# A decoder layer on one core: 15 instead of 11 units of seven block products in the down projection, their row sums formed earlier, residual rows parked in DRAM

## The reference

```
h = h + rmsnorm(merged @ w_out, post_mix_g)          # residual rows, 256 x 2048
u = rmsnorm(h, pre_ffn_g)
ff = (silu(u @ w_gate) * (u @ w_up)) @ w_down        # 2048 -> 5632 -> 2048
h = h + rmsnorm(ff, post_ffn_g)
return h[:, N_META:]                                 # 256 x 2048
```

## Time and profile before

| | |
|---|---|
| median of 3 runs | 1106.71 us (1106.59 to 1107.04) |
| the profiled execution | 1106.06 us |
| its span, first to last instruction | 1104.1 us |
| PE busy | 1090.2 us, 99% |
| DVE busy | 764.0 us, 69% |
| ACT busy | 546.8 us, 50% |
| DMA | 203.52 MB, mean 184 GB/s |
| feed-forward stage, from the first block to the down stage | 368 to 861 us |
| down stage, half 0 | 861 to 978 us |
| down stage, half 1, with the tail | 978 to 1104 us |

### The profile page before, as it was taken

One profiled execution on the slowest core, in us unless ns is written; L12 is line 12 of the kernel. 1 busy time (PEld: TensorE's weight loads), 2 busy tenths in 40 slices (PEclk: granted clock), 3 DMA queues, 4 the chain that ended last, 5 costly groups with the idle time before them and its releaser, 6 DMA issues.

```text
span 1104.1 us, 17760 instructions
## 1 busy us (share of the span) xinstructions
PE 1090.2 (99%) x6479; PEld 968.0 (88%) x6479; DVE 764.0 (69%) x939; ACT 546.8 (50%) x677; POOL 27.3 (2%) x46
## 2 busy tenths in 40 slices
PE   9999999999999999999999999999999999999996
PEld 8999999999888888888888888888888888888885
DVE  6699896546747866666666656666666788787676
ACT  6544544746544754444444444444444455555452
POOL 4001001001000000000000000000000000000000
PEclk9999999999999999999999999999999999999999
DMA  8655445534486376566656666666666656656662
GB/s 279 204 180 162 148 136 152 154 96 153 148 310 191 116 248 190 173 203 190 191 173 198 188 190 184 188 192 190 189 178 197 194 186 205 220 170 215 198 202 95
DMA packets 154847, 203.52 MB, mean 184 GB/s; under 512 B 6305, under 2 KB 133729, under 8 KB 154033
## 3 DMA queue, kind: packets, MB, share of 16 engines
q1 hardware_dynamic: 153616, 197.29, 57.8%
q10 hardware_dynamic: 608, 4.20, 0.9%
q0 software_dynamic: 576, 1.40, 0.4%
HBM read 200.77 MB, written 2.10 MB: 184 GB/s over the span
## 4 chain that ended last, share of the span: by engine, by line
PE 95%; DVE 3%; ACT 1%; issue 0%; DVEq 0%; POOL 0%; ACTq 0%; POOLq 0%
PE ps L1304 29%; PE ps L1306 15%; PE ps L1289 6%; PE ps L1291 5%; PE ps L1292 5%; PE ps L1675 5%; PE ps L1676 5%; PE ps L1677 5%; PE ps L1585 3%; PE ps L1587 3%; PE ps L1586 3%; PE ps L1700 2%; PE ps L1701 2%; PE ps L1702 2%; DVE w_lo L849 1%; PE ps L1443 1%
## 5 line engine op out<-in xcount | busy, mean ns | idle before, releaser
L849 DVE TENSOR_TENSOR w_lo<-raw,w_hi 128x1024 fp32r<-128x1024 f32 x357 | 434.7, 1229 | 252.9 <-ACT w_hi L494 252.2
L494 ACT ACTIVATE w_hi<-raw 128x1024 fp32r<-128x1024 f32 x357 | 375.4, 1059 | 398.0 <-PE ps L1306 253.9
L1304 PE MATMUL ps<-u,w_hi 128*128 128x512 f32 x1408 | 491.1, 392 | 0.8 <-DVE u L957 0.8
L1306 PE MATMUL ps<-u,w_lo 128*128 128x256 f32 x1408 | 395.0, 281 | 0.0
L1304 PEld LDWEIGHTS ps<-u,w_hi 128*128 128x128 f32 x1408 | 264.0, 188 | 60.3 <-issue 1.1
L1306 PEld LDWEIGHTS ps<-u,w_lo 128*128 128x128 f32 x1408 | 265.3, 188 | 0.0
L1289 PE MATMUL ps<-u,w_hi 128*128 128x272 f32 (+1 forms) x544 | 158.8, 292 | 0.0
L1291 PE MATMUL ps<-u,w_hi 128*128 128x272 f32 (+1 forms) x544 | 155.9, 287 | 0.0
L1292 PE MATMUL ps<-u,w_lo 128*128 128x272 f32 (+1 forms) x544 | 155.7, 286 | 0.0
L1675 PE MATMUL ps<-w_hi,ffn 128*128 128x512 f32 x264 | 102.8, 389 | 1.5 <-DVE w_lo L849 1.5
L1289 PEld LDWEIGHTS ps<-u,w_hi 128*128 128x128 f32 x544 | 102.4, 188 | 0.4
(11 more groups left out here) (236 smaller groups left out, 919.3 us busy)
## 6 DMA issues: line engine op xcount, KB each, us to landing
raw<-in_w_gate SPq DMA_DIRECT2D x88, 512.0 KB, 4.6
raw<-in_w_up SPq DMA_DIRECT2D x88, 512.0 KB, 4.5
raw<-in_w_down SPq DMA_DIRECT2D x88, 512.0 KB, 4.7
raw<-in_w_in SPq DMA_DIRECT2D x72, 512.0 KB, 3.6
raw<-in_w_out SPq DMA_DIRECT2D x32, 512.0 KB, 4.5
arena<-in_x SPq DMA_DIRECT2D x2, 1024.0 KB, 6.1
arena<-in_x ACTq DMA_DIRECT2D x2, 1024.0 KB, 8.3
out<-f_acc SPq DMA_DIRECT2D x3, 512.0 KB, 2.7
```

The costliest lines, as they stand in the source:

```text
L494: act.activation(w_hi[:, slot, :], raw[:, slot, :], ACT.Copy).then_inc(hi_done, 1)
L849: dve.tensor_tensor(w_lo[:, slot, :], raw[:, slot, :], hi_view(w_hi[:, slot, :]), ALU.subtract).then_inc(lo_done, 1)
L1304: pe.matmul(ps[:, bank + m, :].rearrange("p (a t) -> p a t", a=2), w_hi[:, slot, at], u[:, kt, :, 0:SEQ], start=first and k == 0, stop=Fal ...
L1306: mm = pe.matmul(ps[:, bank + m, 0:SEQ], w_lo[:, slot, at], u[:, kt, 0, 0:SEQ], start=False, stop=last and k == len(kts) - 1, skip_group_c ...
```

## The change

It has four parts.

1. Which units are seven units, and in what order the units of a half are worked. A string for each half (ROUND, P plain, Z seven) now gives the order, and the list TURNS the unit at each place. Half 0 has seven seven units (before: 5), half 1 has eight (before: 6). Before, they stood at every third place. Now they stand at places 2, 5, 8, 11, 14, 17, 19 of half 0 and 3, 5, 7, 9, 11, 13, 16, 18 of half 1 (places from 0; a place is two chunks). Between most there are two plain units; between 17 and 19 of half 0, and in half 1 between 3, 5, 7, 9, 11, 13 and between 16, 18, there is one.
2. The row sums of units 8 to 12 are made inside feed-forward blocks 8 to 12, from the float32 product tile, in a new tile sums_y. Three sums (units 13, 14, 15) are left in the down stage, before six.
3. sums_y lies over h2rows. The residual rows are therefore written to the output tensor in DRAM (2 MB, two DMAs on ACT's queue) before feed-forward block 1, and read back (two DMAs of 1 MB on SP's queue) when the last seven unit has ended. The load of gbc moves from the beginning of the feed-forward stage to its end.
4. fold_sums stands at place FOLD[n] + 4: 43 in half 0 and 41 in half 1, before 42 in both. SP's loads of w_down are written out, not in a loop.

The core of the diff:

```
-    SEVEN_D = (3, 6, 9, 12, 15, 18)
-    SEVEN_0 = (6, 9, 12, 15, 18)
-    SUM_AT = {4: 6, 9: 9, 15: 12, 21: 15, 27: 18, 33: 3}
+    Y0, Y1 = 8, 13
+    SEVEN_Y, SEVEN_U = tuple(range(Y0, Y1)), (13, 14, 15)
+    SUM_AT = {13: 13, 19: 14, 25: 15}
     SUM_NO = {d: i for i, d in enumerate(SUM_AT.values())}
-    SEVENS = [(n, d) for n in range(DW) for d in (SEVEN_D if n else SEVEN_0)]
+    ROUND = ("PPZPPZPPZPPZPPZPPZPZPP", "PPPZPZPZPZPZPZPPZPZPPP")
+    def in_turn(n):
+        sevens = list(SEVEN_Y + SEVEN_U)[:ROUND[n].count("Z")]
+        plain = [d for d in range(FT // 2) if d not in sevens]
+        return [(sevens if c == "Z" else plain).pop(0) for c in ROUND[n]]
+    TURNS = [in_turn(n) for n in range(DW)]
+    SEVENS = [(n, d) for n in range(DW) for d, c in zip(TURNS[n], ROUND[n]) if c == "Z"]
     SEVEN_NO = {nd: z for z, nd in enumerate(SEVENS)}
     SEVENS_TO = [sum(1 for k, _ in SEVENS if k <= n) for n in range(DW)]
+    SEVEN_END = [ROUND[n].rindex("Z") for n in range(DW)]
     QUARTERS = [(0, 0), (0, 1), (1, 0), (1, 1)]
-    FOLD = 2 * max(SEVEN_D) + 2
-    assert FOLD <= DCH - LAST and 0 not in SEVEN_D and DW == 2
+    FOLD = [2 * SEVEN_END[n] + 1 for n in range(DW)]
...
-        sums = sb_at("sums", [P, len(SEVEN_D), 3, 2, P], F32R, a_sums)
-        assert 4 * NQ * WIDE <= 24 * P * len(SEVEN_D) <= a_in + 8 * KT * TOK - a_sums
+        sums = sb_at("sums", [P, len(SEVEN_U), 3, 2, P], F32R, a_sums)
...
+        y_f = sb_at("y_f", [P, 1, 4, P], F32, a_xt)
...
+        sums_y = sb_at("sums_y", [P, Y1 - Y0, 3, 2, P], F32R, a_y)
...
-            with sp_eng.Fori(0, DW) as i:
-                for kt in range(DCH):
-                    load(wd_v, kt, i * WIDE, i * DCH + (Q_DOWN + kt), kt % WSLOTS, kts=1, cols=WIDE)
+            for n in range(DW):
+                for e in range(DCH):
+                    q = Q_DOWN + n * DCH + e
+                    load(wd_v, 2 * TURNS[n][e // 2] + e % 2, n * WIDE, q, q % WSLOTS, kts=1, cols=WIDE)
+            sp_eng.wait_ge(h2_kept, 16 * NQ)
+            sp_eng.wait_ge(t_used, len(SEVENS))
+            for m in range(NQ):
+                sp_eng.dma_start(h2rows[:, m, :], out_v[:, m, :]).then_inc(h2_back[m], 16)
...
-            act.wait_ge(y_sq, NQ * DN)
-            act.wait_ge(yg_done, NQ * DN)
-            act.dma_start(gbc[:, :], post_ffn_g.to_broadcast([P, D])).then_inc(gbc_landed, 16)
...
+            act.wait_ge(rows_done, NQ * DN)
+            for m in range(NQ):
+                act.dma_start(out_v[:, m, :], h2rows[:, m, :]).then_inc(h2_kept, 16)
...
+            with act.Fori(1, Y0) as i:
+                gate_part(i)
+                up_part(i, range(CK, 2 * CK))
+            act.wait_ge(h2_kept, 16 * NQ)
+            with act.Fori(0, Y1 - Y0) as j:
+                gate_part(j + Y0)
+                up_part(j + Y0, range(CK, CK + 2))
+                act.wait_ge(y_step, j * 4 + 4)
+                act.copy(sums_y[:, bass.ds(j, 1), :, 0, :], y_f[:, :, 0:3, :]).then_inc(y_hi, 1)
+                act.copy(ffn[:, bass.ds(j * 2 + 2 * Y0, 1), 0, P:SEQ], y_f[:, 0, 3:4, :]).then_inc(y_hi, 1)
+                up_part(j + Y0, range(CK + 2, 2 * CK))
+            with act.Fori(Y1, NFB - 1) as i:
+                gate_part(i)
+                up_part(i, range(CK, 2 * CK))
+            act.wait_ge(y_lo, 2 * (Y1 - Y0))
+            act.dma_start(gbc[:, :], post_ffn_g.to_broadcast([P, D])).then_inc(gbc_landed, 16)
...
+            def product_sums(j):
+                a11, a12, a21, a22 = (tmp_ffn[:, 3, k * SEQ + m * P:k * SEQ + (m + 1) * P] for m in range(2) for k in range(2))
+                dve.tensor_tensor(y_f[:, 0, 0, :], a21, a22, ALU.add).then_inc(y_step, 1)
+                dve.tensor_tensor(y_f[:, 0, 3, :], a11, a21, ALU.subtract).then_inc(y_step, 1)
+                dve.wait_ge(y_step, j * 4 + 1)
+                dve.tensor_tensor(y_f[:, 0, 1, :], y_f[:, 0, 0, :], a11, ALU.subtract).then_inc(y_step, 1)
+                dve.wait_ge(y_step, j * 4 + 3)
+                dve.tensor_tensor(y_f[:, 0, 2, :], a12, y_f[:, 0, 1, :], ALU.subtract).then_inc(y_step, 1)
+            def product_sums_lo(j):
+                dve.wait_ge(y_step, j * 4 + 4)
+                dve.wait_ge(y_hi, j * 2 + 2)
+                dve.wait_ge(f_lo, j + Y0 + 1)
+                dve.tensor_tensor(sums_y[:, bass.ds(j, 1), :, 1, :], y_f[:, :, 0:3, :],
+                                  hi_view(sums_y[:, bass.ds(j, 1), :, 0, :]), ALU.subtract).then_inc(y_lo, 1)
+                at = bass.ds(j * 2 + 2 * Y0, 1)
+                dve.tensor_tensor(ffn[:, at, 1, P:SEQ], y_f[:, 0, 3:4, :], hi_view(ffn[:, at, 0, P:SEQ]),
+                                  ALU.subtract).then_inc(y_lo, 1)
+            with dve.Fori(1, Y0) as i:
+                gate_part(i)
+                up_part(i, range(CK))
+            dve.wait_ge(h2_kept, 16 * NQ)
+            dve.wait_ge(y_sq, NQ * DN)
+            dve.wait_ge(yg_done, NQ * DN)
+            with dve.Fori(0, Y1 - Y0) as j:
+                gate_part(j + Y0)
+                product_sums(j)
+                up_part(j + Y0, range(3))
+                product_sums_lo(j)
+                up_part(j + Y0, range(3, CK))
+            dve.wait_ge(y_lo, 2 * (Y1 - Y0))
+            with dve.Fori(Y1, NFB - 1) as i:
...
+                    dve.wait_ge(h2_back[m], 16)
...
-            def seven_products(n, d):
-                z, i, q = SEVEN_NO[n, d], SUM_NO[d], Q_DOWN + n * DCH + 2 * d
+            def seven_products(n, e):
+                d, q = TURNS[n][e // 2], Q_DOWN + n * DCH + e
+                z = SEVEN_NO[n, d]
...
+                    if d in SEVEN_Y:
+                        return [sums_y[:, d - Y0, s, h, :] for h in range(2)]
+                    return [sums[:, SUM_NO[d], s, h, :] for h in range(2)]
```

More of the change, by code:

```diff
@@ L323, in build_trunk @@
         t_made, t_hi_done, t_lo_done, t_used, s_step, s_hi, s_lo, x0_kept, x_step, fold_done, x_hi, x_lo, \
[L324 to L325 removed]
+            ident_rounded, y_step, y_hi, y_lo, h2_kept, h2_back0, h2_back1 = (sem(n) for n in ("t_made", "t_hi_done", "t_lo_done", "t_used", "s_step", "s_hi", "s_lo",
+                                              "x0_kept", "x_step", "fold_done", "x_hi", "x_lo", "ident_rounded", "y_step", "y_hi",
+                                              "y_lo", "h2_kept", "h2_back0", "h2_back1"))
+        h2_back = [h2_back0, h2_back1]
         def tiles(w):
@@ L768, in _, with gate_part @@
             silu0 = Q_FFN + 2 * CK
-            with act.Fori(1, NFB - 1) as i:
+            def gate_part(i):
                 keep_low(i, 0, Q_FFN + CK)
@@ L775, in _, with up_part @@
                 keep_low(i, 1, Q_FFN + 2 * CK)
-                for s in range(CK, 2 * CK):
+            def up_part(i, steps):
+                for s in steps:
                     split_hi(i * 2 * CK + (silu0 + s), s % WSLOTS, i * 2 + (silu0 + s) // WSLOTS)
+            with act.Fori(1, Y0) as i:
[14 more added lines that the diff above has]
+            act.dma_start(gbc[:, :], post_ffn_g.to_broadcast([P, D])).then_inc(gbc_landed, 16)
             keep_low(NFB - 1, 0, Q_FFN + CK)
@@ L811, in _ @@
                 if n < DW:
-                    z = SEVEN_NO.get((n, e // 2))
+                    z = SEVEN_NO.get((n, TURNS[n][e // 2]))
                     if z is None:
@@ L827, in _ @@
                 n, e = (q - 4 - Q_DOWN) // DCH, (q - 4 - Q_DOWN) % DCH
-                if q - 4 >= Q_DOWN and e == FOLD:
+                if q - 4 >= Q_DOWN and e == FOLD[n]:
                     act.wait_ge(t_used, SEVENS_TO[n])
@@ L1139, in _, with gate_part @@
                 split(Q_FFN + 2 * CK + s)
-            with dve.Fori(1, NFB - 1) as i:
+            def gate_part(i):
                 gate_evac(i)
@@ L1144, in _, with up_part @@
                 up_evac(i)
-                for s in range(CK):
+            def up_part(i, steps):
+                for s in steps:
                     split_lo(i * 2 * CK + (Q_FFN + 3 * CK + s), s)
+            def product_sums(j):
[29 more added lines that the diff above has]
+            with dve.Fori(Y1, NFB - 1) as i:
+                gate_part(i)
+                up_part(i, range(CK))
             gate_evac(NFB - 1)
@@ L1673, in down_products @@
                     rows_m, mv = slice(m * P, (m + 1) * P), slice(j * DCOLS, (j + 1) * DCOLS)
-                    first, last = kt == 0, kt == DCH - 1
+                    first, last = e == 0, e == DCH - 1
                     pe.matmul(o, ffn[:, kt, 0, rows_m], w_hi[:, slot, mv], start=first, stop=False)
@@ L1723, in _ @@
                 whole = DCH if n < DW - 1 else DCH - LAST
[L1724 to L1728, removed]
+                for e in range(whole):
+                    if (n, TURNS[n][e // 2]) not in SEVEN_NO:
+                        down_products(n, e, QUARTERS).then_inc(chunks_used, 1)
+                    elif e % 2 == 0:
+                        seven_products(n, e)
             for m, j in QUARTERS:
-                for kt in range(DCH - LAST, DCH):
```

(3 more changed lines are left out.)

19 lines of the change are left out of this document (12 added, 7 removed).

## The result

| | before | changed kernel |
|---|---|---|
| median, us | 1106.68 (1106.59 to 1107.04, 4 runs) | 1114.14 (1112.21 to 1115.08, 4 runs) |
| profiled execution, us | 1106.06 | 1115.08 |
| its span, us | 1104.1 | 1113.2 |

The ratio is 1.0064 [1.0051, 1.0076]: slower, as forecast, but by 7.5 us and not by 3.4, and above the top of the range (1112.9). The profiled execution is the slowest of the four; its trace tells where its 9.0 us are, not what each execution loses.

A forecast was written before the change was run, and what follows sets the result against it. The prediction took PE to bound the kernel: -2.72 (matmuls) + 6.02 (seven turns) + 1.14 (opening) - 1.06 (end of half 1) = +3.38 us, giving a median of 1110.1 us, range 1106.8 to 1112.9.

The forecast's parts named there:

- The kernel is bound by PE, 12 matmuls are 2.72 us: Whole kernel: PE bounds everything; four more seven units save three matmuls each at 0.2267 us, 2.72 us less.
- The chain from t_used and its 6.63 us: Down stage: DVE's seven-unit work waits for t_used, then takes 6.63 us; PE loses 0.86 us a turn, 6.02 over seven.
- Rival A: Down-stage loop does not wait, mean load decides (8.91 us against 10.20), only the opening is late: 1104.1 us; 8%.
- Rival B: Down-stage handoffs overlap with work, a turn costs the low bound of 0.51 us: 1107.6 us, no change that shows; 16%.
- DVE starts 0.42 us after the start of the matmul that it waits for: Down-stage loop: handoff from PE's last matmul of a seven unit to DVE's first weight sum, 0.42 us of the turn's 11.06.
- The usual one is just in time, and I take 0.86: Down-stage loop: the usual second-chunk load, 4.1 us, meets DVE's need after 4.43 us, so a turn loses 0.86 us.
- rival C: Down-stage loop: the load, not t_used, ends last; a turn loses 1.38 us: 1112.2, or 1116.6 with 5.8 us loads; 11%.
- The three row sums less in the down stage take load off DVE where it waited anyway: nothing: Down stage: three fewer row sums on DVE were claimed to change nothing in the time.
- The opening: First seven unit of half 0, at place 2: DVE's chain ends late for product 2, PE loses 1.14 us.
- The end of half 1: Tail: with fold_sums ahead of chunk 42, PE's one wait shrinks, giving back 1.06 us.
- What costs nothing: Sums in blocks 8 to 12, fewer down-stage row sums, the rows' way back and the loop cut in three: no cost.
- Rival D: Early feed-forward stage: parked rows hold up weight loads, up to 3.7 us lost at chunk 115: 1113.8 us; 8%.

The follow-up runs named there:

- e7: The order of e2 with sixteen seven units, eight in half 0, and down-stage row sums at chunks 7, 13, 19, against e2: 1102.66 us.
- e2: The changed kernel with the second chunk's parts made ahead of the weight sums' parts, on ACT and DVE: 1103.34 us.
- e6: The kernel before with only e2's edit, the second chunk's parts ahead of the weight sums' parts: 1106.8 us.
- e1: The changed kernel with unit 15 worked as the first plain unit of half 0, not at place 12: 1112.42 us.
- e4: The kernel before with fold_sums of half 1 at place 41 and not 42, nothing else: 1105.6 us.
- e5: The changed kernel with twelve seven units, two plain units between all, and one row sum in the down stage: 1106.72 us.

## Why the prediction was right and wrong

- **The kernel is bound by PE, 12 matmuls are 2.72 us: right.** e7 shows the same rate again (three matmuls, 0.68 us).
- **The chain from t_used and its 6.63 us: right**, and shown by e2 and e6: with the second low part ahead of the t_lo the stops go, and where the slack is large the same edit does nothing. Rival A, by which mean load decides, is out in the changed kernel: DVE is busy 70% and PE stands all the same. After e2's edit PE no longer stands in the loop. Rival B (0.51 a turn) is out too.
- **"DVE starts 0.42 us after the start of the matmul that it waits for": mis-sized.** The 0.42 came from another pair of instructions, the sum of a quarter in PSUM; the weight sums start 0.53 behind. With small parts a turn loses 0.98 and not 0.86 us: 7 x 0.12 = 0.8 us.
- **"The usual one is just in time, and I take 0.86": the step that failed most.** The prediction had the cover in hand, 4.43 us, and had seen one load of 5.8 us in the earlier trace rows, and put the late load into rival C as an all or nothing, four turns or none. Its "usual" load of 4.1 us was one row; the median of its own rows, 4.7, is over the cover. In the run the cover held six times, for these loads took 3.5 to 4.1 us, and failed once, at 6.0. What came was one turn of seven, in the traces of the changed kernel and of e1: 1.54 us in one, 0.98 in the other. Rival C's own working, 0.25 + 5.8 + 6.63 = 12.68 us for such a turn, is what the trace has (12.74). A term for one load as slow as the slowest of the earlier trace rows falling into the loop belonged in the sum.
- **Behind it the clock: a step that was missing.** No term allowed for PE running slower once it had stood. 1.5 us in the profiled execution, none in e1's.
- **The wait queued behind the row sums of unit 15: missed.** "The three row sums less in the down stage take load off DVE where it waited anyway: nothing" looked at the sums that went, not at what the ones that stayed now wait for. Unit 15's tile is used late in half 0 in the new order of turns. 1.05 us, shown by e1, where it goes.
- **The opening: right** (1.14 and 1.13 us; PE at product 2 12.6 us behind the stage's start, 861.72 to 874.35).
- **The end of half 1: right** (-1.06 and -1.07 us; e4 alone -1.0).
- **What costs nothing: right** but for 0.07 us at 394 us (e5). Rival D, which had up to 3.7 us there, is out: the feed-forward stage has no wait of PE.

So the direction and the mechanism of the turn stood, and the sum was short of a late load, a stop and the low clock. Of the 5.6 us of difference in the profiled execution 3.1 are the one turn with the late load and the low clock, 1.05 unit 15's wait, 0.7 the handoff in the other turns, and 0.7 small parts. The median is 4.0 over the forecast. The executions of the changed kernel lie at 1112.2 and at 1113.9 to 1115.1, those of e1 at 1111.6 to 1112.4 and at 1114.3 (twice). Of the two profiled, the upper had the low clock and the lower had not. That it is so in the others isn't shown: the low clock alone was worth 1.5 us, and e1's execution of 1114.26 us has a mean granted clock of 0.998, as its profiled one of 1112.42 without the low stretch, where the changed kernel's profiled one has 0.996. What parts the two groups stays open.

## What to carry to other kernels

Where two engines hand one buffer back and forth, work out the turn (last use, handoff, the chain up to the piece that is needed first, handoff), not the mean load, and put first in the chain what the other engine reads first: here the parts of one chunk changed places with those of the weight sums, and 7 us of loss became 3 us of gain. This loop had about 1 us in hand against its load, and one load in seven missed it by 1.5 us; where a trace of before shows loads slower than the cover, price one into the sum, and the low clock that may follow a long stop with it. When the order of work changes, go through every wait that stayed, for what it waits for may have moved.

## What the hardware showed that was not expected

**A late load beside a long packet of instructions.** In the changed kernel and in e1 the late load ran beside a packet of instructions of 2.6 us, and in before the load of 5.8 us of the earlier trace rows (issued at 955.0) did too:

```profile
q8 instruction: 1, 0.02, 13.1%
```

(before, 955.9 to 957 us: 0.131 x 16 x 1.1 = 2.3 us.) The mean over all 31 such packets of the changed kernel is near 1.1 us (0.2% of 16 engines' 1113 us). In the down stages of the nine traces no other such packet took 2 us or more, and a load issued at 1052.46, 0.4 us behind the start of a packet of 0.9 us, took 3.7. But this is a coincidence in time: no run took the packet away, and one cause may have drawn out both. The case of before is the weakest, for its loads of the down stage took up to 7.0 us with no long packet beside them. The Trainium skill, page "DMA: Bandwidth & Descriptors", section "Queues, rings and completion order", says that a DMA engine takes turns between its queues a whole packet at a time; by that one long packet holds up the sixteenth of the load that goes through the same engine, and the load lands with its last part. The amounts in the changed kernel agree with it (6.0 us against 3.5, beside 2.6 us of packet); which engine carried the packet no row shows.

**PE's clock after a stop.** With nothing started between 1029.30 and 1031.94 us the granted clock was 0.50 from 1032 to 1035 us; in e1 the stop from 1028.74 to 1030.82 left it up. At the low clock the steps were 0.43 us. The Trainium skill, page "TensorE: Matmul & The Clock Gate", section "Wait — 56ns, not 53.3ns?", gives 426.7 ns for 512 columns there, and the trace agrees.
